# Moving the running sum of squares of a pre-norm from VectorE to GpSimd in a two-part transformer kernel

## The reference, cut to what matters

```
def rms_norm(x, g):
    x32 = x.astype(jnp.float32)
    y = x32 * lax.rsqrt(jnp.mean(x32 * x32, axis=-1, keepdims=True) + RMS_EPS)
    return (y * g.astype(jnp.float32)).astype(x.dtype)

# in each layer of the second kind, for block = ffn, mixer, ffn, gated embedding:
h = h + rms_norm(block(rms_norm(h, g_pre)), g_post)
```

## Time and profile before

| | |
|---|---|
| median of 3 runs | 3431.12 us |
| the profiled execution | 3430.66 us |
| its span in the trace | 3428.8 us |
| mean granted clock of TensorE | 0.988 of full |
| running sum on VectorE (L2104) | 56 additions, 38.4 us busy |
| sums of the post-norms on GpSimd (L677) | 45 additions, 60.8 us busy |

### The profile page before, as it was taken

The page is one execution under the profiler, slowest core; times in us unless marked ns, Lnnn a source line. Parts: engine busy times, 40 slices in busy tenths (PEclk is TensorE's granted clock), DMA queues, the critical chain, the costliest instruction groups (busy, mean ns, idle before and its releaser), DMA issues.

```text
span 3428.8 us, 42531 instructions
## 1 busy us (share of the span) xinstructions
PE 3317.4 (97%) x16570; PEld 2633.9 (77%) x16570; DVE 1836.8 (54%) x2932; ACT 1241.6 (36%) x1878; POOL 342.3 (10%) x244
## 2 busy tenths in 40 slices
PE   9999999999899999999999999999999989999997
PEld 6667888776688887888777778887788876688886
DVE  5776334567752446443566664435644357654436
ACT  3354222424442324332333342324432235532324
POOL 0310000212100020000233100000000012100001
PEclk9999999999999999999999999999999999999999
DMA  4102222311122222223322122232222321122232
GB/s 162 62 32 74 96 95 98 128 62 50 50 85 94 98 98 81 98 97 104 107 74 68 63 81 96 98 105 93 86 96 94 105 94 39 61 98 98 98 105 80
DMA packets 81431, 300.35 MB, mean 88 GB/s; under 512 B 9040, under 2 KB 9040, under 8 KB 80640
## 3 DMA queue, kind: packets, MB, share of 16 engines
q1 hardware_dynamic: 78624, 284.20, 24.8%
q0 software_dynamic: 1568, 11.98, 0.9%
q10 hardware_dynamic: 1088, 2.10, 0.2%
HBM read 296.14 MB, written 2.10 MB: 87 GB/s over the span
## 4 chain that ended last, share of the span: by engine, by line
PE 88%; DVE 6%; ACT 3%; issue 1%; POOL 1%; DMA 1%; ACTq 0%; DVEq 0%; POOLq 0%
PE bank L874 25%; PE bank L876 25%; PE bank L875 24%; PE bank L918 2%; PE bank L925 2%; PE bank L919 2%; DVE wl L2026 1%; PE bank L1411 1%; ACT sc L1710 1%; PE bank L1423 1%; PE bank L1175 1%; PE bank L1156 1%; ACT wh L1549 1%; PE bank L1466 1%; PE bank L1114 1%
## 5 line engine op out<-in xcount | busy, mean ns | idle before, releaser
L874 PE MATMUL bank<-x,wh 128*128 128x512 f32 x2632 | 1053.7, 400 | 14.8 <-DVE h L2470 5.7
L876 PE MATMUL bank<-x,wl 128*128 128x512 f32 x2632 | 1027.3, 390 | 0.0
L875 PE MATMUL bank<-x,wh 128*128 128x512 f32 x2632 | 1026.1, 390 | 0.0
L1549 ACT ACTIVATE wh<-raw 128x1024 fp32r<-128x1024 f32 x528 | 558.0, 1057 | 1171.6 <-PE bank L876 1083.6
L2026 DVE TENSOR_TENSOR wl<-raw,wh 128x1024 fp32r<-128x1024 f32 x528 | 677.7, 1284 | 567.4 <-ACT wh L1549 566.0
L874 PEld LDWEIGHTS bank<-x,wh 128*128 128x128 f32 x2632 | 494.9, 188 | 135.9 <-issue 29.4
L876 PEld LDWEIGHTS bank<-x,wl 128*128 128x128 f32 x2632 | 494.6, 188 | 105.4
L875 PEld LDWEIGHTS bank<-x,wh 128*128 128x128 f32 x2632 | 495.7, 188 | 98.4 <-issue 3.4
L874 PE MATMUL bank<-mid,wh 128*128 128x512 f32 x1216 | 474.9, 391 | 0.5 <-DVE wl L2026 0.5
L876 PE MATMUL bank<-mid,wl 128*128 128x512 f32 x1216 | 473.1, 389 | 0.0
L875 PE MATMUL bank<-mid,wh 128*128 128x512 f32 x1216 | 473.1, 389 | 0.0
(11 more groups left out here) (340 smaller groups left out, 3294.5 us busy)
## 6 DMA issues: line engine op xcount, KB each, us to landing
raw<-stream SPq DMA_DIRECT2D x528, 512.0 KB, 3.3
raw_apart<-stream SPq DMA_DIRECT2D x10, 512.0 KB, 3.6
sm<-small POOLq DMA_DIRECT2D x2, 2144.0 KB, 10.6
tb<-tab POOLq DMA_DIRECT2D x2, 1728.0 KB, 14.8
h<-x_t ACTq DMA_DIRECT2D x4, 512.0 KB, 6.8
out_t<-h SPq DMA_DIRECT2D x8, 256.0 KB, 2.1
tba<-tab_a POOLq DMA_DIRECT2D x1, 1152.0 KB, 8.5
pf<-p_t POOLq DMA_DIRECT2D x2, 512.0 KB, 3.9
```

What stands on the lines that cost most here:

```text
L874: pe.matmul(dst, hi, src[:, kc, 0, :], start=start, stop=False)
L875: pe.matmul(dst, hi, src[:, kc, 1, :], start=False, stop=False)
L876: return pe.matmul(dst, lo, src[:, kc, 0, :], start=False, stop=stop)
L1549: act.activation(high_of(n)[:, :], raw_of(n)[:, :], ACT.Copy).then_inc(hi_done, 1)
```

## The change

`add_square` is removed from VectorE. GpSimd gets a function `pre_squares` that makes the same 7 additions a section from the same buffers into the same acc, with the same semaphores. It is called once for each of the 8 sections, at the place in GpSimd's order where the section lies. It first waits until the last sum in acc was read (stat_done), then for each square. The wait for sq_used ahead of the load of pf is dropped, since GpSimd's own additions now come before it. VectorE only counts on its semaphore totals.

```diff
+            def pre_squares():
+                pool.wait_ge(stat_done, c.n["stats"])
+                c.wait(sq_made)
+                for k in range(1, DC):
+                    c.wait(sq_made)
+                    both = 2 if k == 1 else 1
+                    pool.tensor_tensor(acc[:, :], sq[0][:, :] if k == 1 else acc[:, :], sq[k % 2][:, :],
+                                       ALU.add).then_inc(sq_used, both)
+                    c.wait(sq_used, both)
...
                 pool.dma_start(tb[:, 2 * S:], tab[:, 2 * S:]).then_inc(mask_in, 16)
+                pre_squares()
                 c.start(banks_gated)
...
                 u += (40, 20)[layer]
-
-                pool.wait_ge(sq_used, DC * (2 * DEPTH + 4 * layer + 3))
+                pre_squares()
                 pool.dma_start(pf[:, :, :], p_t[layer].rearrange("(c p) t -> p c t", p=P)).then_inc(p_in, 16)
                 square_sums()
+                pre_squares()
...
                 square_sums()
+                if layer < DEPTH - 1:
+                    pre_squares()
...
-                    if not to_x:
-                        add_square(k)
-                        if k + 3 < DC:
-                            centre(k + 3)
+                    if not to_x and k + 3 < DC:
+                        centre(k + 3)
+                if not to_x:
+                    c.tick("sq_made", DC)
+                    c.tick("sq_used", DC)
...
-            def add_square(k):
-
-                if k:
-                    both = 2 if k == 1 else 1
-                    c.wait(sq_made, both)
-                    dve.tensor_tensor(acc[:, :], sq[0][:, :] if k == 1 else acc[:, :], sq[k % 2][:, :],
-                                      ALU.add).then_inc(sq_used, both)
-                    c.wait(sq_used, both)
...
                     if k + 2 < DC:
                         part(k + 2)
-                    add_square(k)
                     if then is not None:
                         then(k)
+                c.tick("sq_made", DC)
+                c.tick("sq_used", DC)
                 begin()
```

## The result

The changed kernel took 3441.99 us (median of 8 runs, 3438.55 to 3442.81) against 3431.2 us for the kernel before (8 runs): a ratio of 1.0029 with a 95% interval of 1.002 to 1.0038. The prediction was 3442.3, with a range of 3435 to 3454. The profiled execution has a span of 3440.3 us against 3428.8, 11.5 us more.

A forecast was written before the change was run, and what follows sets the result against it. The matmul engine, busy 97% of the span, was taken as the bound. Five sections 8.6, embedding sections 2.1 and clock 0.9 gave 11.6 us; 3430.66 + 11.6 = 3442.3, range 3435 to 3454.

The forecast's parts named there:

- Bound and lead: Five residual sections: matmul engine never waits after its start; high parts lead by 1.63 to 2.86 us, together 10.9.
- Taking turns: Section chunks: VectorE and GpSimd instructions reading SBUF alternate whole; residual add 1.7 to 1.8 us, chunk 3.26 against 2.66.
- The reason for 3.9: Delay of chunk 7's high part: 4.1 us if GpSimd goes first, 3.1 if VectorE; 3.9 taken, as GpSimd leads by 0.04.
- the first tie: Chunk of 1673.41: GpSimd's addition would start at 1674.04 or slightly later, VectorE's residual add at 1674.08, nearly a tie.
- A sign that came out otherwise: Sections at 1671 and 1987: matmul waits for the high part in chunks 4 to 7, about 1.2 and 2.3 us in all.
- LayerNorm section: Section at 1303: its lead of 4.47 us exceeds the whole 4.1 us delay, so no loss.
- Embedding sections: Two sections: the 2.04 us wait for a weight split grows about 1.0 us each, together +2.1.
- The clock term: Second embedding section: a 3 us wait makes the slow clock (1.7 us) likelier; at even chances +0.9 us.
- The last addition: Section ends: it ends 1.95 us behind the last high part, its matmul stands 2.2 behind; hidden by 0.2 us.
- No turns taken: Rival: residual add stays 0.69 us beside GpSimd; −2.4 to −4.1 us, 3426.6 to 3428.3; chance 0.07 including any gain.
- The leads hide it: Rival: VectorE wins near ties, five sections lose 4.6 us or less; total 2.8 to 6.4, 3433 to 3437; chance 0.15.
- the small waits: Rival: matmul waits of some 0.5 us in last chunks lower the clock; five sections lose 8.5 more, 3450.8; chance 0.10.

The follow-up runs named there:

- the run with the five sections alone: Against the changed kernel, VectorE again makes the sum in the LayerNorm and embedding sections, GpSimd only in the five residual ones; 3441.64 us, ratio 1.0025 to the kernel before.
- the run with the added wait: Changed kernel plus one GpSimd wait: addition k starts only after VectorE's residual add of chunk k+1; 3432.03 us, ratio 1.0003 to the kernel before.
- one-column: Changed kernel with GpSimd's 56 additions cut to one column each, sum of squares not computed; 3424.94 us, ratio 0.9980 to the kernel before.
- write-only: Changed kernel with each GpSimd addition replaced by three memsets of acc, sum not computed; 3427.55 us, ratio 0.9990 to the kernel before.

## Why the prediction was right

- **Bound and lead.** The matmul engine is the bound, with leads of 1.63 to 2.86 us in the five sections. The losses by the leads are 3.80 − 2.68 = 1.12 (1.17 measured), 3.80 − 1.63 = 2.17 (2.24), 1.95 (2.01), 0.94 (1.05), 1.94 (2.00). This is an agreement within one pair of traces. The sum of the five sections, where VectorE doesn't set them, was 108.0 to 110.0 us over seven traces, by how long the clock was low; where it does, 117.4 in both. So the loss can be 7.4 to 9.5 us by the execution that it is compared with, and 8.5 is one draw.
- **Taking turns.** Read from the earlier trace rows and right: the residual add took 1.8 us, the chunk 3.26 as worked out. The reason for 3.9 held only in part: the first tie, 0.04 us apart on paper, fell to VectorE in all five sections. The next addition started 0.33 us ahead of the residual add and the four behind it 0.03 to 0.05, and these five went to GpSimd. The delay of 3.8 us lies between the bounds of 3.1 and 4.1 and next to the 3.9 that was taken. The five sections: 8.6 forecast, 8.5 measured.
- **A sign that came out otherwise.** Waits for the high part of about 1.2 and 2.3 us in all were named for the sections at 1671 and 1987. The profile's brackets have 0.48 and 0.43 (twice 0.24; 0.22 and 0.21), in the last two chunks alone. They count from the end of a record of 0.39 us, and the next matmul would start 0.23 us after the last one's start, so that such a wait costs more than its bracket; the lengths of the sections show the loss, 1.17 and 2.24.
- **ScalarE.** Its square of chunk 2 was not free of the addition, as was said: it waited some 0.42 us for GpSimd's first one in each of the five sections.
- **LayerNorm section.** Nothing forecast, 0.03 us measured.
- **Embedding sections.** The sign was right, the size of the term wasn't: the wait grew by 0.69 us, not 1.0. The part that was too small is what two additions free in the queue: 1.2 was taken, but from the start of an addition to the start of what follows it pass 0.73 and 0.72 us (2360.14 to 2360.87, 2362.80 to 2363.52 before), 1.45 in all. Two instructions were held, by 1.05 and 1.09 us as forecast, though the first was a product and not a residual add: 2.14 − 1.45 = 0.69. The term of 2.1 should have been 1.4; with only this part undone the sections were 1.2 shorter. The clock term (+0.9) looked confirmed in the one trace, where the second embedding section grew by 1.45 us beyond its longer wait and had a clock of 0.93 instead of 1.00. But the run with the five sections alone had the slow stretch in both embedding sections without any longer wait, and the run with the added wait had it in one only (0.93 and 1.00) behind waits of 2.7 us. It comes and goes between executions, and no run shows that the change brings it. The five alone came out at 9.9 us by medians where their traces say 8.5, so the total agreed better than its terms deserve: each term is known to 1 or 2 us, and a total within 0.3 us of the median is luck.
- **The last addition** stayed hidden: the matmul for the sum follows 2.2 us behind the last high part (1693.09 to 1695.34), the addition ended at 1695.05.
- **Rivals.** "No turns taken" would have had the residual add at 0.69; the one-column and the write-only runs show what it would have given, 3425 to 3428, near the 3426.6 to 3428.3 of its sum. "The leads hide it" is what came true for the five sections with the added wait. The clock wasn't brought down by the small waits: the windows of the changed kernel over the second halves of the five sections all have a granted clock of 1.00; two of them:

```profile
1682.00:1696.00 14.00, 13.52 (x58) 10.19 (x56) 10.70 (x11) 5.90 (x9) 5.17 (x5) 1.00 0.00 1
2002.00:2013.00 11.00, 10.57 (x45) 7.90 (x44) 8.30 (x8) 4.21 (x7) 4.79 (x5) 1.00 0.00 0
```

## What to carry to other kernels

Before work is moved from VectorE to GpSimd, look what VectorE does at that moment. Here its instructions read two operands in SBUF, and it wasn't relieved but held to the end of each addition on GpSimd, which takes nearly twice as long as VectorE's own. The price is set by which instruction is held and how much lead the bound engine has there; ordering GpSimd behind the instruction on the critical chain, with one wait, took back the whole loss of the five sections, and no difference to the kernel before was left that could be measured (1.0003, 0.9994 to 1.0012). And read the bound engine's real waits first: moving one weight split by a chunk was worth 6 us, while moving 38 us of additions off VectorE made VectorE busier by 14.5.

## What the runs showed of the hardware

- An instruction on either side is held to the end of the other's, not slowed in proportion: a residual add ended 0.55 us after GpSimd's addition, and its duration follows the other's (1.22 beside 0.74, 1.80 beside 1.29: 0.5 more each time).
- Starts 0.03 to 0.05 us apart in the records went with GpSimd going first, in four chunks of each of the five sections; at 0.01 us VectorE went first, in all five, although its record starts later.
- Beside GpSimd's addition a VectorE instruction with one operand in PSUM took 0.68 us, and the next, with both in SBUF, 1.19 instead of 0.69.
- GpSimd's memset of 128x512 took 0.53 us and held VectorE not at all (residual add 0.684 us in the median, as without GpSimd), although three of them lasted longer than the addition.
- The same wait of 2.04 us ended in a stretch at the lower clock in three embedding sections (22.3 us long) and not in a fourth (20.6), which moves a section by 1.6 us between executions of kernels that are alike there. Differences of that size in a single trace prove nothing.
